# Gate products of all rows ahead of the last expert block's down product

## The chip, the cores and the metric

One core of a Trainium2 chip runs the whole program. The metric is the device time of one execution in microseconds, on that core.

## What is computed

One decoder layer on 320 rows of width 1024 (256 prompt rows and 64 sample rows): attention-like mixers, then a mixture of experts, then the per-layer input embedding, then a last norm. Everything is float32. The change touches what follows the last expert block:

```python
x = x + _moe(_rms(x, norm_moe_g[i]), router_w[i], ...)      # top 4 of 32 experts, clamped SwiGLU
gate = jax.nn.sigmoid(_rms(x, norm_ple_g[i]).astype(x.dtype) @ ple_gate_w[i])
x = x + gate * (p[i] @ ple_w[i])
...
y = _rms(x, final_norm_g)
```

`_rms` multiplies each row by one number (one over the root of its mean square) and each column by a gain. So `_rms(x) @ W` is, row by row, that number times `(x * gain) @ W`, and `(x * gain) @ W` is a sum over the parts of which `x` is made.

## The kernel before, in words

The 320 rows stand in `X` as three tiles: t = 0 and t = 1 with 128 prompt rows each, t = 2 with the 64 sample rows. The experts are walked in blocks of up to 64 rows (`SL`), one after the other, on a ring of 12 weight slots of 1 MB. A block's up and gate weights take slots 0 to 7 (four transfers of 2 MB), its down weights slots 8 to 11 (two transfers). Each body of the loop, `expert(i + 2, 2)`, does on TensorE the up product of block b, the scatter of block b-2, the gather of block b+1 and the down product of block b-1. SyncE's queue issues each transfer as soon as the semaphore `w_used` says that its slots have been read.

Scatter: a block's result `yS` holds 64 rows in 128 partitions (columns 0 to 511 of a row in partition s, columns 512 to 1023 in partition 64 + s). `SELT` holds the router's weights as a selection matrix, so `SELT^T @ yS` adds each row of the block, times its weight, to the row of `X` it belongs to.

Behind the loop stands the tail, with last_b the last block. Its up product has been done by then, its down product not. On TensorE the tail is, in this order: the sums for block last_b-1 and for the bias (`sum_slots`, `sum_bias`, L1192 and L1199) that stay open in six PSUM banks, the turn of the selection (L1093), the down product of last_b from slots 0 to 3 (L1133), its scatter into the same open banks (L1221), then for the tiles in `LAST_ORDER` = (2, 0, 1) the transposes of `X` (L568) and the products with the gate weights `wple` (L1244 for t = 2, L1232 for t = 0 and t = 1). VectorE adds the banks to `X` (L2204) and writes the transposes, times the gain, to `xT` (L2213). ScalarE takes the sums of squares (L1268), and GpSimd the power -0.5 (L453).

The rest of the tail goes over six halves (three tiles, two halves of 512 columns): ScalarE takes the sigmoid of a gate bank (L1557), VectorE multiplies it with the embedding part `pw` (L2229) and adds it to `X` (L2231). After both halves of a tile ScalarE squares the tile (L1268, or L1563 by halves for t = 1), GpSimd takes the power, VectorE scales the rows (L2236, L2243), and SyncE stores them. ScalarE and VectorE work strictly in the order written: the sigmoid of tile 0 stands behind the squares of tile 2 on ScalarE, and the products of tile 0 stand behind the last scaling of tile 2 on VectorE.

Of the kernel before, what the change touches and what calls it, by code (L numbers as in the profile page):

```python
# [12 lines left out]
P = 128  # L13
# [14 lines left out]
NE = 32  # L28
# [28 lines left out]
def build(nc, a, o):  # L57
    with ExitStack() as ctx:
# [103 lines left out]
        wple = ring[:, 8 * SLOTW:12 * SLOTW].rearrange("p (k n) -> p k n", k=KD)  # L162
# [63 lines left out]
        gT = etake(NTOK)  # L226
        bdr = xT[:, :, :].rearrange("p c t -> p (c t)")[0:NE, 0:D]
# [64 lines left out]
        TAKEN = {"pT": 1, "lexp": 2, "gT": 3}  # L292
# [5 lines left out]
        def _(sp):  # L298
# [82 lines left out]
            with sp.Fori(0, rest) as i:  # L381
                b = i + 1
                e = sp.value_load(etab[0:1, bass.ds(b + 1, 1)], min_val=0, max_val=NE - 1)
                for c in range(0, NGU, 2):
                    sp.wait_ge(sem("w_used"), used(b, c + 1))
                    load_pair(sp, e, c)
                e = sp.value_load(etab[0:1, bass.ds(b, 1)], min_val=0, max_val=NE - 1)
                for c in range(NGU, NCK, 2):
                    sp.wait_ge(sem("w_used"), used(b, c + 1))
                    load_pair(sp, e, c)  # L390
            e = sp.value_load(etab[0:1, bass.ds(last_b, 1)], min_val=0, max_val=NE - 1)
# [3 lines left out]
            w_ple = a["ple_gate_w"].rearrange("o (k p) n -> p (o k) n", p=P)  # L395
# [135 lines left out]
        def _(pe):  # L531
# [657 lines left out]
            def sum_slots(t, start, stop):  # L1189

                for h in range(2):
                    last = mm(PB[SUMB[t][h]][0:ROWS[t], :], SELT[SL * h:SL * h + SL, OFF[t]:OFF[t] + ROWS[t]],  # L1192
                              yS[SL * h:SL * h + SL, :], start=start, stop=stop, skip_group_check=True)
                return last

            def sum_bias(t):

                for n in range(2):
                    mm(PB[SUMB[t][n]][0:ROWS[t], :], gT[0:NE, OFF[t]:OFF[t] + ROWS[t]], bdr[:, 512 * n:512 * n + 512],  # L1199
                       start=False, stop=False, skip_group_check=True)  # L1200
# [6 lines left out]
            for t in (0, 2):  # L1207
                sum_slots(t, True, False)
                sum_bias(t)
            pe.wait_ge(sem("xg"), last_b + 2)  # L1210
            pe.wait_ge(sem("up"), last_b + 1)
            sum_slots(1, True, False)
            sum_bias(1)
            turn_select(last_b, 2)
            pe.wait_ge(sem("act"), last_b + 1)
            for c in range(NGU, NCK):
                down_chunk(last_b, c, c - NGU)
            pe.wait_ge(sem("selT"), last_b + 1)
            pe.wait_ge(sem("yS"), last_b + 1)
            for t, h in ((0, 0), (2, 0), (2, 1), (0, 1), (1, 0), (1, 1)):  # L1220
                last = mm(PB[SUMB[t][h]][0:ROWS[t], :], SELT[SL * h:SL * h + SL, OFF[t]:OFF[t] + ROWS[t]],  # L1221
                          yS[SL * h:SL * h + SL, :], start=False, stop=True, skip_group_check=True)
                if (t, h) in ((2, 1), (0, 1), (1, 1)):
                    last.then_inc(sem("x2_ps"), 1)

            def ple_gate(t):

                R = ROWS[t]
                pe.wait_ge(sem("xT"), 14 + 2 * t + 2)
                for n in range(2):  # L1230
                    for k in range(KD):
                        last = mm(PB[SUMB[t][n]][0:R, :], xT[:, k, OFF[t]:OFF[t] + R], wple[:, k, 512 * n:512 * n + 512],  # L1232
                                  start=(k == 0), stop=(k == KD - 1))
                    last.then_inc(sem("gate_ps"), 1)

            pe.wait_ge(sem("x1"), 8)
            turn_rows_x(2, (2, 4))
            pe.wait_ge(sem("x1"), 10)
            pe.wait_ge(sem("xT"), 14)
            turn_rows_x(0, (2, 4))  # L1240
            pe.wait_ge(sem("ple_in"), 64)
            for k in range(KD):
                for n in range(2):
                    last = mm(PB[0][64 * n:64 * n + 64, :], xT[:, k, 256:320], wple[:, k, 512 * n:512 * n + 512],  # L1244
                              start=(k == 0), stop=(k == KD - 1), skip_group_check=True)
            last.then_inc(sem("gate_ps"), 2)
# [3 lines left out]
            ple_gate(0)  # L1250
            ple_gate(1)
# [3 lines left out]
        def _(act):  # L1255
# [284 lines left out]
            take_select(last_b, 2)  # L1540
# [27 lines left out]
        def _(dve):  # L1568
# [628 lines left out]
            def add_last(i):  # L2197
# [17 lines left out]

            add_last(0)
            add_last(1)
            xT_last(0)
            xT_last(1)
            add_last(2)  # L2220
            xT_last(2)
            for i in range(3):
# [50 lines left out]
```

## Time and profile before

| | |
|---|---|
| median of 3 runs | 1320.37 us (1319.15 to 1327.6) |
| profiled execution, its own time | 1324.6 us |
| span of its trace | 1322.9 us |
| TensorE busy | 1260.6 us, 95% of the span |
| VectorE busy | 522.6 us, 40% |
| ScalarE busy | 214.6 us, 16% |
| DMA, over the span | 438.30 MB, mean 331 GB/s |
| granted TensorE clock, mean | 0.993 of full speed |

Starts are counted from the first instruction of the span. A matmul of this program stands in the trace as two records, so "x32" is 16 matmuls. Busy times of TensorE are modelled at their ends, so a start to the next start is the surer length.

### The profile page before, as it was taken

How to read it: one execution, taken by the hardware profiler on the slowest of the kernel's cores; microseconds unless marked ns; L12 is line 12 of the kernel's file. 1: busy time of each engine (PE TensorE's matmuls, PEld its weight loads, DVE VectorE, ACT ScalarE, POOL GpSimd, SP SyncE). 2: the span in 40 equal slices, each digit the busy share in tenths (PEclk: the TensorE clock that was granted, in tenths of full speed). 3: DMA queues.
4: the chain of work that ended last, by engine and by line, in shares of the span. 5: the costliest groups of instructions: out<-in, count | busy, mean ns of one | idle time of the engine just before them, and what ended most of it. 6: DMA issues, size and time to landing. Idle time of an engine off the chain costs nothing.

```text
span 1322.9 us, 17013 instructions
## 1 busy us (share of the span) xinstructions
PE 1260.6 (95%) x6271; PEld 546.7 (41%) x6271; DVE 522.6 (40%) x1148; ACT 214.6 (16%) x422; POOL 46.7 (4%) x106
## 2 busy tenths in 40 slices
PE   6999898889999999999999999999999999999997
PEld 4765687644333333333333333333333333333333
DVE  2683444745833334343333333333334333333333
ACT  2451102142111111111111111111111111111112
POOL 5100001100000000000000000000000000000000
PEclk9999999989999999999999999999999999999999
DMA  8431110346799999999999999999999999999931
GB/s 246 119 114 64 64 65 5 135 170 228 281 427 427 429 430 428 429 428 429 428 430 429 428 429 428 429 429 429 428 428 429 430 428 429 428 428 429 430 152 40
DMA packets 54485, 438.30 MB, mean 331 GB/s; under 512 B 10538, under 2 KB 17863, under 8 KB 29850
## 3 DMA queue, kind: packets, MB, share of 16 engines
q1 hardware_dynamic: 54336, 437.89, 80.0%
q8 instruction: 18, 0.29, 0.1%
q14 instruction: 9, 0.07, 0.0%
q10 hardware_dynamic: 122, 0.04, 0.0%
HBM read 432.89 MB, written 5.02 MB: 331 GB/s over the span
## 4 chain that ended last, share of the span: by engine, by line
PE 52%; DMA 41%; DVE 3%; issue 2%; ACT 1%; POOL 0%; SPq 0%; DVEq 0%; POOLq 0%; ACTq 0%
DMA ring<-in_expert_w_down 40%; PE bank L1122 12%; PE bank L1133 12%; PE bank L597 8%; PE bank L1078 2%; PE bank L773 2%; PE bank L595 2%; PE bank L1108 1%; PE bank L1232 1%; PE bank L682 1%; PE bank L694 1%; PE bank L1143 1%; PE bank L692 1%; DMA X<-in_x_sample 1%; PE bank L1086 1%
## 5 line engine op out<-in xcount | busy, mean ns | idle before, releaser
L1122 PE MATMUL bank<-ring,SC 128*64 128x512 f32 x2048 | 465.1, 598 | 13.3 <-DMA ring<-in_expert_w_gu 12.3
L1122 PEld LDWEIGHTS bank<-ring,SC 128*64 128x64 f32 x2048 | 140.4, 137 | 303.8 <-issue 267.7
L1133 PE MATMUL bank<-ring,SC 128*64 128x512 f32 x1024 | 229.9, 594 | 3.9 <-DMA ring<-in_expert_w_down 3.9
L2091 DVE TENSOR_TENSOR SC<-bank,gmoe 128x512 f32<-128x512 f32 x33 | 22.8, 692 | 464.7 <-PE bank L1086 464.6
L1133 PEld LDWEIGHTS bank<-ring,SC 128*64 128x64 f32 x1024 | 71.5, 137 | 156.4 <-issue 133.2
L2109 DVE TENSOR_TENSOR X<-X,bank 128x512 f32<-128x512 f32 x120 | 77.1, 684 | 106.1 <-PE bank L1108 105.1
L597 PE MATMUL bank<-xT,ring 128*128 128x320 f32 x384 | 112.5, 440 | 6.6 <-ACTq L1330 5.6
L1499 ACT ACTIVATE SC<-bank 128x512 f32<-128x512 f32 x33 | 19.7, 597 | 448.6 <-PE bank L1078 448.6
L1078 PE MATMUL bank<-XS,SC 128*64 128x512 f32 x396 | 90.6, 592 | 0.6 <-DVE SC L2085 0.6
L597 PEld LDWEIGHTS bank<-xT,ring 128*128 128x128 f32 x384 | 70.7, 191 | 35.9 <-ACTq L1330 7.5
L1108 PE MATMUL bank<-SC 64*128 64x512 f32 x240 | 67.7, 641 | 0.0
L2122 DVE TENSOR_TENSOR SC<-bank,bgu 128x256 f32<-128x256 f32 x128 | 48.1, 418 | 11.9 <-issue 10.8
L1078 PEld LDWEIGHTS bank<-XS,SC 128*64 128x64 f32 x396 | 28.4, 137 | 57.5 <-issue 47.4
L2113 DVE TENSOR_TENSOR X<-X,bank 64x256 f32<-64x256 f32 x120 | 49.9, 416 | 1.8
L1512 ACT ACTIVATE SC<-bank 128x512 f32<-128x512 f32 x31 | 18.5, 598 | 187.8 <-PE bank L1133 187.8
L453 POOL TENSOR_TENSOR nst<-nst,mhalf 128x1 f32<-128x1 f32 (+1 forms) x12 | 6.5, 542 | 1035.0 <-DVE nst L1594 1014.3
L1143 PE MATMUL bank<-ident,SC 128*128 128x128 f32 x256 | 36.1, 284 | 0.5 <-ACT SC L1504 0.5
L773 PE MATMUL bank<-ring,xT 128*128 128x512 f32 x64 | 33.2, 652 | 1.2 <-DVE X L1609 0.8
L1503 ACT ACTIVATE SC<-bank 128x512 f32<-128x512 f32 x32 | 19.1, 597 | 90.8 <-PE bank L1122 90.8
L1143 PEld LDWEIGHTS bank<-ident,SC 128*128 128x128 f32 x256 | 33.3, 208 | 0.7 <-ACT SC L1504 0.7
L1108 PEld LDWEIGHTS bank<-SC 64*128 64x128 f32 x240 | 18.1, 184 | 35.9 <-issue 35.9
L1516 ACT ACTIVATE SC<-SC 128x512 f32<-128x512 f32 x32 | 20.1, 630 | 68.3 <-DVE SC L2130 68.3
(478 smaller groups left out, 1019.9 us busy)
## 6 DMA issues: line engine op xcount, KB each, us to landing
ring<-in_expert_w_gu SPq DMA_DIRECT2D x128, 2048.0 KB, 23.3
ring<-in_expert_w_down SPq DMA_DIRECT2D x64, 2048.0 KB, 24.4
ring<-in_w_in SPq DMA_DIRECT2D x7, 2048.0 KB, 7.8
ring<-in_w_out SPq DMA_DIRECT2D x2, 2048.0 KB, 8.4
ring<-in_ple_gate_w SPq DMA_DIRECT2D x4, 1024.0 KB, 15.2
out_gdn_s<-Sf SPq DMA_DIRECT2D x1, 2048.0 KB, 9.4
X<-in_x_prompt SPq DMA_DIRECT2D x2, 512.0 KB, 6.4
SC<-in_ple_w SPq DMA_DIRECT2D x1, 1024.0 KB, 5.0
```

The lines of the kernel that those rows point to most:

```text
L595: ins = mm(out[0:ROWS[c], :], xT[:, k, OFF[c]:OFF[c] + ROWS[c]], w[:, k, :], start=(k == 0), stop=(k == KD - 1))
L597: ins = mm(out[:, 0:NTOK], w[:, k, c * P:c * P + P], xT[:, k, :], start=(k == 0), stop=(k == KD - 1))
L773: ins = mm(PB[0][:, :], xT[:, k, OFF[t]:OFF[t] + P], wo[:, k, 512 * n:512 * n + 512], start=(k == 0), stop=(k == KD - 1))
L1078: last = mm(PB[7][SL * h:SL * h + SL, :], SEL[:, t, :], XS[:, t, 512 * h:512 * h + 512], start=(t == 0), stop=(t == 2), skip_group_check=True)
L1108: last = mm(out[:, :], SELT[SL * h:SL * h + SL, P * t:P * t + P], yS[SL * h:SL * h + SL, :], start=True, stop=True)
L1122: last = mm(PB[j][SL * h:SL * h + SL, :], xg[:, c % 4, c // 4, :], w[:, FF * h + 512 * j:FF * h + 512 * j + 512], start=(c == 0), stop=(c ...
L1133: last = mm(PB[4][SL * h:SL * h + SL, :], act_t[:, 2 * (c - NGU) + kk, :], w[:, D * kk + 512 * h:D * kk + 512 * h + 512], start=(c == NGU ...
L1143: last = turn(PB[2 + m // 4][:, P * (m % 4):P * (m % 4) + P], hS[:, spread(m, 4)], ident[:, :])
L2091: tell(V.tensor_tensor(xg, PB[7][:, :].rearrange("p (j h s) -> p j h s", j=4, h=2), bc(gmoe[:, :, :].rearrange("p h j -> p j h"), 3, SL), ...
L2109: ins = V.tensor_tensor(dst, dst, src[0:R, :], ALU.add)
L2113: ins = V.tensor_tensor(dst, dst, src[64 * r:64 * r + 64, 0:256], ALU.add)
L2122: ins = V.tensor_tensor(out[:, 4 * i:4 * i + 4, :], PB[2 + i][:, :].rearrange("p (k h s) -> p k h s", k=4, h=2)[:, :, h, :], bgu[:, c0 + 4 ...
```

## The change

The gate product is split. `X` gets the share of all blocks but the last, is transposed and multiplied with `wple` while the last block's down product hasn't been done. Then the down product follows, and its share is added on two ways: to `X` by the scatter, as before, and to the open gate banks by transposing `yS` to `yT`, multiplying its 64 rows with `wple` (a result `zS` of 64 rows) and scattering `zS` with the same `SELT`.

On TensorE there are 26 matmuls more: four transposes of `yS`, 16 for `yT` with `wple`, and six to scatter `zS`. VectorE gets one more pass from a PSUM bank (`yT`) and six more adds to `X` (`add_part`, over all three tiles, stands beside `add_last`), ScalarE one more copy (`zS`). `wple` moves from slots 8 to 11 to slots 0 to 3 and is loaded first, as two transfers of 2 MB in the place of four of 1 MB; the last down weights go to slots 8 to 11 behind it.

```diff
-        wple = ring[:, 8 * SLOTW:12 * SLOTW].rearrange("p (k n) -> p k n", k=KD)
+        wple = ring[:, 0:4 * SLOTW].rearrange("p (k n) -> p k n", k=KD)
...
+        yT = gt.rearrange("p k s -> p (k s)").rearrange("p (j h s) -> p j h s", j=4, h=2)
+        zS = hS[:, 0:512]
...
+            for i in range(2):
+                sp.wait_ge(sem("w_used"), used(last_b, 2 * i + 1))
+                sp.dma_start(wple[:, 4 * i:4 * i + 4, :], w_ple[:, 4 * i:4 * i + 4, :]).then_inc(sem("ple_in"), 16)
             e = sp.value_load(etab[0:1, bass.ds(last_b, 1)], min_val=0, max_val=NE - 1)
-            for i in range(0, NDN, 2):
-                sp.wait_ge(sem("w_used"), used(last_b, i + 1))
-                sp.dma_start(ring[:, i * SLOTW:(i + 2) * SLOTW], w_dn[e, :, i // 2, :]).then_inc(sem(f"w_full{i}"), 16)
...
-            for i in range(NDN):
-                sp.wait_ge(sem("w_used"), used(last_b, NGU + i))
-                sp.dma_start(wple[:, 2 * i:2 * i + 2, :], w_ple[:, 2 * i:2 * i + 2, :]).then_inc(sem("ple_in"), 16)
+            for c in range(NGU, NCK, 2):
+                sp.wait_ge(sem("w_used"), used(last_b, c + 1))
+                load_pair(sp, e, c)
...
+            sum_slots(0)
+            sum_slots(2)
+            sum_bias(2).then_inc(sem("x2_ps"), 1)
+            sum_bias(0).then_inc(sem("x2_ps"), 1)
...
+            sum_slots(1)
+            sum_bias(1).then_inc(sem("x2_ps"), 1)
+
+            def gate_half(t, n):
+
+                for k in range(KD):
+                    mm(PB[SUMB[t][n]][0:ROWS[t], :], xT[:, k, OFF[t]:OFF[t] + ROWS[t]], wple[:, k, 512 * n:512 * n + 512],
+                       start=(k == 0), stop=False, skip_group_check=True)
+
+            def last_rows(t, banks):
+
+                for h in range(2):
+                    out = PB[banks[h]][0:P, :] if t < 2 else PB[banks[0]][SL * h:SL * h + SL, :]
+                    last = mm(out, SELT[SL * h:SL * h + SL, OFF[t]:OFF[t] + ROWS[t]], yS[SL * h:SL * h + SL, :],
+                              start=True, stop=True, skip_group_check=True)
+                last.then_inc(sem("x2_ps"), 1)
...
             pe.wait_ge(sem("x1"), 12)
             pe.wait_ge(sem("xT"), 16)
             turn_rows_x(1, (2, 4))
-            ple_gate(0)
-            ple_gate(1)
+            gate_half(0, 0)
+            gate_half(0, 1)
+            pe.wait_ge(sem("xT"), 18)
+            down(last_b)
+            gate_half(1, 0)
+            pe.wait_ge(sem("selT"), last_b + 1)
+            pe.wait_ge(sem("yS"), last_b + 1)
+            for j in range(4):
+                last = turn(PB[1][:, P * j:P * j + P], yS[:, P * j:P * j + P], ident[:, :])
+            last.then_inc(sem("xsT"), 1)
+            last_rows(2, (4,))
+            gate_half(1, 1)
+            pe.wait_ge(sem("xT"), 19)
+            last_rows(0, (1, 2))
+            pe.wait_ge(sem("x1"), 14)
+            for k in range(KD):
+                for n in range(2):
+                    last = mm(PB[4][SL * n:SL * n + SL, :], yT[:, k % 4, k // 4, :], wple[:, k, 512 * n:512 * n + 512],
+                              start=(k == 0), stop=(k == KD - 1), skip_group_check=True)
+            last.then_inc(sem("gate_ps"), 1)
+            pe.wait_ge(sem("x1"), 16)
+            last_rows(1, (1, 2))
+            pe.wait_ge(sem("taken"), TAKEN["zS"])
+            for t in LAST_ORDER:
+                for n in range(2):
+                    out = PB[SUMB[t][n]][0:P, :] if t < 2 else PB[0][SL * n:SL * n + SL, :]
+                    last = mm(out, SELT[SL * n:SL * n + SL, OFF[t]:OFF[t] + ROWS[t]], zS[SL * n:SL * n + SL, :],
+                              start=False, stop=True, skip_group_check=True)
+                    if t < 2:
+                        last.then_inc(sem("gate_ps"), 1)
+                if t == 2:
+                    last.then_inc(sem("gate_ps"), 2)
...
             for i in range(3):
+                if i == 2:
+                    act.wait_ge(sem("gate_ps"), 1)
+                    A(zS, PB[4][:, :], ACT.Copy).then_inc(sem("taken"), 1)
                 t = LAST_ORDER[i]
-                act.wait_ge(sem("x1"), 6 + 2 * i + 2)
+                act.wait_ge(sem("x1"), 12 + 2 * i + 2)
                 squares(t, XS[:, t, :]).then_inc(sem("ss"), 1)
...
-                act.wait_ge(sem("gate_ps"), i + 1)
+                act.wait_ge(sem("gate_ps"), i + 2)
...
+            dve.wait_ge(sem("xsT"), 19)
+            tell(V.tensor_tensor(yT, PB[1][:, :].rearrange("p (j h s) -> p j h s", j=4, h=2),
+                                 bc(pcol[:, 16:24].rearrange("p (h j) -> p j h", h=2), 3, SL), ALU.mult), "xT")
+            add_last(0, (4,))
+            add_last(1, (1, 2))
+            add_last(2, (1, 2))
```

TensorE around the last down product. In the kernel before it stands behind the turn of the selection, and its scatter (L1221) right behind it:

```order
L1093 MATMUL bank2<-ident,SC 128x128 [waits selg]
L1093 MATMUL bank2<-ident,SC 128x128 x2
L1129 ISA [waits act]
L1133 MATMUL bank4<-ring,SC 64x512 [waits w_full0]
L1133 MATMUL bank4<-ring,SC 64x512 x7
L1133 MATMUL bank4<-ring,SC 64x512 [waits w_full2]
L1133 MATMUL bank4<-ring,SC 64x512 x7
L1221 MATMUL bank5<-SC 128x512 [waits yS,selT]
L1221 MATMUL bank0<-SC 64x512
L1221 MATMUL bank1<-SC 64x512
L1221 MATMUL bank6<-SC 128x512
L1221 MATMUL bank7<-SC 128x512
```

In the changed kernel (its own line numbers: L1221 is now a half of a gate product, L1228 the scatter of the last block's rows, L1254 the transposes of `yS`):

```order
L1221 MATMUL bank5<-ring,xT 128x512 x8
L1221 MATMUL bank6<-ring,xT 128x512 x8
L1131 ISA [waits act,xT]
L1135 MATMUL bank4<-ring,SC 64x512 [waits w_full8]
L1135 MATMUL bank4<-ring,SC 64x512 x7
L1135 MATMUL bank4<-ring,SC 64x512 [waits w_full10]
L1135 MATMUL bank4<-ring,SC 64x512 x7
L1221 MATMUL bank7<-ring,xT 128x512 x8
L1254 MATMUL bank1<-ident,SC 128x128 [waits yS,selT]
L1254 MATMUL bank1<-ident,SC 128x128 x3
L1228 MATMUL bank4<-SC 64x512 x2
L1221 MATMUL bank3<-ring,xT 128x512 x8
```

The down product now stands behind the gate product of tile 0 and ahead of both halves of tile 1's. TensorE's last rows, in the kernel before, from the last transposes on:

```order
L568 MATMUL bank2<-ident,X 128x128 [waits xT,x1]
L568 MATMUL bank2<-ident,X 128x128 x3
L568 MATMUL bank4<-ident,X 128x128 x4
L1232 MATMUL bank5<-ring,xT 128x512 [waits xT]
L1232 MATMUL bank5<-ring,xT 128x512 x7
L1232 MATMUL bank6<-ring,xT 128x512 x8
L1232 MATMUL bank7<-ring,xT 128x512 [waits xT]
L1232 MATMUL bank7<-ring,xT 128x512 x7
L1232 MATMUL bank3<-ring,xT 128x512 x8
```

In the changed kernel (L1263 is `yT` with `wple`, L1272 the scatter of `zS`):

```order
L1228 MATMUL bank1<-SC 128x512 [waits xT]
L1228 MATMUL bank2<-SC 128x512
L1263 MATMUL bank4<-ring,SC 64x512 [waits x1]
L1263 MATMUL bank4<-ring,SC 64x512 x15
L1228 MATMUL bank1<-SC 128x512 [waits x1]
L1228 MATMUL bank2<-SC 128x512
L1272 MATMUL bank0<-SC 64x512 [waits taken]
L1272 MATMUL bank0<-SC 64x512
L1272 MATMUL bank5<-SC 128x512
L1272 MATMUL bank6<-SC 128x512
L1272 MATMUL bank7<-SC 128x512
L1272 MATMUL bank3<-SC 128x512
```

The gate banks 0, 5, 6, 7 and 3 are now completed all together at the very end, where each was completed by its own product. ScalarE, from its copy of `yS` on, before:

```order
L1542 ACTIVATE SC<-bank4 128x512 [waits w_used]
L1268 ACTIVATE XS,nst<-X 64x1024 [waits x1]
L1268 ACTIVATE XS,nst<-X 128x1024 [waits x1] x2
L1557 ACTIVATE SC<-bank0,nst 64x512 [waits rs,gate_ps] x2
L1268 ACTIVATE XS,nst<-X 64x1024 [waits x3]
L1557 ACTIVATE SC<-bank5,nst 128x512 [waits x3,rs,gate_ps]
L1557 ACTIVATE SC<-bank6,nst 128x512 [waits x3,rs,gate_ps]
L1268 ACTIVATE XS,nst<-X 128x1024 [waits x3]
L1557 ACTIVATE SC<-bank7,nst 128x512 [waits x3,rs,gate_ps]
L1563 ACTIVATE XS,nst<-X 128x512 [waits x3]
L1557 ACTIVATE SC<-bank3,nst 128x512 [waits x3,rs,gate_ps]
L1563 ACTIVATE XS,nst<-X 128x512 [waits x3]
```

And in the changed kernel (L1568 the copy of `yS`, L1574 that of `zS`, L1294 the squares, L1586 the sigmoids, L1592 the squares by halves):

```order
L1568 ACTIVATE SC<-bank4 128x512 [waits w_used]
L1294 ACTIVATE XS,nst<-X 64x1024 [waits x1]
L1294 ACTIVATE XS,nst<-X 128x1024 [waits x1]
L1574 ACTIVATE SC<-bank4 128x512 [waits gate_ps]
L1294 ACTIVATE XS,nst<-X 128x1024 [waits x1]
L1586 ACTIVATE SC<-bank0,nst 64x512 [waits rs,gate_ps] x2
L1294 ACTIVATE XS,nst<-X 64x1024 [waits x3]
L1586 ACTIVATE SC<-bank5,nst 128x512 [waits x3,rs,gate_ps]
L1586 ACTIVATE SC<-bank6,nst 128x512 [waits x3,rs,gate_ps]
L1294 ACTIVATE XS,nst<-X 128x1024 [waits x3]
L1586 ACTIVATE SC<-bank7,nst 128x512 [waits x3,rs,gate_ps]
L1592 ACTIVATE XS,nst<-X 128x512 [waits x3]
```

The sigmoids stand in the same order, but the copy of `zS` and the squares of tile 1 ahead of the first of them now wait for the end of TensorE's row.

## Rows read from the trace of the kernel before

**Rows 1.** The page's chain that ended last: shares of the span by engine.
```profile
PE 52%; DMA 41%; DVE 3%; issue 2%; ACT 1%; POOL 0%; SPq 0%; DVEq 0%; POOLq 0%; ACTq 0%
```

**Rows 2.** The chain in order of time, from 1220.91 on: start, us, link, instructions.
```profile
1220.91 3.68 PE bank L1133 x16
1224.74 25.50 DMA ring<-in_expert_w_down
1250.28 3.65 PE bank L1133 x16
```

**Rows 3.** Stretches of the tail: busy time and instructions by engine, clock, DMA share, GB/s.
```profile
core 0: us, PE busy (x) PEld busy (x) DVE busy (x) ACT busy (x) POOL busy (x), PEclk, DMA share, GB/s
1268.00:1272.00 4.00, 4.00 (x20) 1.15 (x16) 0.00 (x0) 0.00 (x0) 0.00 (x0) 1.00 0.34 129
1265.00:1315.00 50.00, 47.96 (x166) 19.92 (x164) 16.65 (x29) 10.99 (x19) 2.62 (x5) 1.00 0.14 51
1315.05:1322.90 7.85, 0.00 (x0) 0.00 (x0) 3.01 (x5) 1.39 (x3) 0.54 (x1) 0.77 0.18 67
```

**Rows 4.** Timeline, TensorE in the tail: start, us, line, operation, idle time before it.
```profile
1255.83 1.13 PE L1192 MATMUL bank<-SC 64*128 64x512 f32 x4
...
1256.89 1.98 PE L1199 MATMUL bank<-xT,SC 32*128 32x512 f32 x4
...
1264.63 0.55 PE L1093 MATMUL bank<-ident,SC 128*128 128x128 f32 x3
...
1265.11 7.09 PE L1133 MATMUL bank<-ring,SC 128*64 128x512 f32 x32
...
1272.98 4.01 PE L1221 MATMUL bank<-SC 64*128 64x512 f32 x12 [0.79 <-ACT SC L1542]
...
1276.46 0.71 PE L568 MATMUL bank<-ident,X 64*128 64x64 f32 x8
...
1278.41 1.07 PE L568 MATMUL bank<-ident,X 128*128 128x128 f32 x8 [1.25 <-DVE xT L2213]
...
1279.41 7.09 PE L1244 MATMUL bank<-ring,xT 128*64 128x512 f32 x32
...
1286.43 1.09 PE L568 MATMUL bank<-ident,X 128*128 128x128 f32 x8
...
1287.36 27.63 PE L1232 MATMUL bank<-ring,xT 128*128 128x512 f32 x64
```

**Rows 5.** Timeline, VectorE and ScalarE between 1259 and 1283.
```profile
1259.89 0.85 DVE L2098 TENSOR_SCALAR SC<-iota_s,posb,gateb 128x128 f32<-128x128 f32 x3
...
1272.24 0.60 ACT L1542 ACTIVATE SC<-bank 128x512 f32<-128x512 f32 x1 [6.54 <-PE bank L1133]
...
1280.29 1.27 DVE L2204 TENSOR_TENSOR X<-X,bank 128x512 f32<-128x512 f32 x2
...
1281.59 1.06 ACT L1268 ACTIVATE XS<-X 128x1024 f32<-128x1024 f32 x1 [2.81 <-DVE X L2204]
...
1282.56 0.19 ACT L1268 ACTIVATION_READ_ACCUMULATOR XS<-X 128x1 f32 x1
```

**Rows 6.** Timeline, VectorE and ScalarE from the first sigmoid on.
```profile
1289.18 1.39 ACT L1557 ACTIVATE SC<-bank,nst 64x512 f32<-64x512 f32 x2 [6.43 <-POOL nst L453]
...
1295.82 0.68 DVE L2229 TENSOR_TENSOR SC<-SC,Sf 128x512 f32<-128x512 f32 x1
...
1296.54 0.69 DVE L2231 TENSOR_TENSOR X<-X,SC 128x512 f32<-128x512 f32 x1
...
1303.47 1.06 ACT L1268 ACTIVATE XS<-X 128x1024 f32<-128x1024 f32 x1 [1.49 <-DVE X L2231]
...
1305.45 1.28 DVE L2236 SCALAR_TENSOR_TENSOR X<-X,nst,ring 128x1024 f32<-128x1024 f32 x1 [0.65 <-POOL nst L453]
...
1310.33 0.63 ACT L1563 ACTIVATE XS<-X 128x512 f32<-128x512 f32 x1 [1.49 <-DVE X L2231]
...
1315.03 0.69 ACT L1557 ACTIVATE SC<-bank,nst 128x512 f32<-128x512 f32 x1 [3.97 <-PE bank L1232]
```

More of the change, by code:

```diff
@@ L1187, in _, with sum_slots @@
             SUMB = [(5, 6), (7, 3), (0, 1)]
-            def sum_slots(t, start, stop):
+            def sum_slots(t):
                 for h in range(2):
-                    last = mm(PB[SUMB[t][h]][0:ROWS[t], :], SELT[SL * h:SL * h + SL, OFF[t]:OFF[t] + ROWS[t]],
-                              yS[SL * h:SL * h + SL, :], start=start, stop=stop, skip_group_check=True)
-                return last
+                    mm(PB[SUMB[t][h]][0:ROWS[t], :], SELT[SL * h:SL * h + SL, OFF[t]:OFF[t] + ROWS[t]],
+                       yS[SL * h:SL * h + SL, :], start=True, stop=False, skip_group_check=True)
             def sum_bias(t):
                 for n in range(2):
-                    mm(PB[SUMB[t][n]][0:ROWS[t], :], gT[0:NE, OFF[t]:OFF[t] + ROWS[t]], bdr[:, 512 * n:512 * n + 512],
-                       start=False, stop=False, skip_group_check=True)
+                    last = mm(PB[SUMB[t][n]][0:ROWS[t], :], gT[0:NE, OFF[t]:OFF[t] + ROWS[t]], bdr[:, 512 * n:512 * n + 512],
+                              start=False, stop=True, skip_group_check=True)
+                return last
             pe.wait_ge(sem("selT"), rest + 1)
@@ L1216, in _ @@
[L1216 to L1234, printed above, removed]
+            sum_slots(1)
+            sum_bias(1).then_inc(sem("x2_ps"), 1)
@@ L1236, in _ @@
             pe.wait_ge(sem("x1"), 8)
             turn_rows_x(2, (2, 4))
+            turn_select(last_b, 1)
             pe.wait_ge(sem("x1"), 10)
@@ L1240, in _ @@
             turn_rows_x(0, (2, 4))
-            pe.wait_ge(sem("ple_in"), 64)
+            pe.wait_ge(sem("ple_in"), 32)
             for k in range(KD):
                 for n in range(2):
-                    last = mm(PB[0][64 * n:64 * n + 64, :], xT[:, k, 256:320], wple[:, k, 512 * n:512 * n + 512],
-                              start=(k == 0), stop=(k == KD - 1), skip_group_check=True)
-            last.then_inc(sem("gate_ps"), 2)
+                    mm(PB[0][64 * n:64 * n + 64, :], xT[:, k, 256:320], wple[:, k, 512 * n:512 * n + 512],
+                       start=(k == 0), stop=False, skip_group_check=True)
             pe.wait_ge(sem("x1"), 12)
@@ L2195, in _, with add_part @@
             SUMB = [(5, 6), (7, 3), (0, 1)]
-            def add_last(i):
+            def add_part(i):
                 t = LAST_ORDER[i]
@@ L2204, in add_last @@
                     tell(V.tensor_tensor(dst, dst, PB[SUMB[t][n]][0:R, :], ALU.add), "x1")
+            def add_last(i, banks):
+                t = LAST_ORDER[i]
+                R = ROWS[t]
+                dve.wait_ge(sem("x2_ps"), 3 * rest + 3 + i + 1)
+                for n in range(2):
+                    src = PB[banks[n]][0:P, :] if t < 2 else PB[banks[0]][SL * n:SL * n + SL, :]
+                    dst = X[0:R, t, 512 * n:512 * n + 512]
+                    tell(V.tensor_tensor(dst, dst, src, ALU.add), "x1")
             def xT_last(i):
@@ L2214, in xT_last @@
                                          bc(pcol[:, 16 + 4 * hb:16 + 4 * hb + 4], 2, R), ALU.mult), "xT")
-            add_last(0)
-            add_last(1)
+            add_part(0)
+            add_part(1)
             xT_last(0)
+            add_part(2)
             xT_last(1)
-            add_last(2)
             xT_last(2)
+            dve.wait_ge(sem("xsT"), 19)
[4 more added lines that the diff above has]
+            add_last(2, (1, 2))
             for i in range(3):
```

14 lines of the change are left out of this document (4 added, 10 removed).

## The prediction

> **What bounds the kernel now.** I read the page's chain first: TensorE has 52% of the span and the DMA 41% [rows 1]. Followed in order of time, the chain shows where each rules. Up to 1250.28 it alternates between 25.50 us of weight transfer and 3.65 to 3.68 us of down product [rows 2]: the expert loop is paced by the weights. The step at 1250.28 is the last one in it that has a transfer as its link. The question for this change is whether TensorE stands idle in the tail for want of weights, because that idle time is what gate products set ahead of the last down product could fill. So next the stretches: the DMA stream falls to a share of 0.34 between 1268 and 1272, so it ends near 1269, and TensorE is busy for 4.00 of those 4.00 us [rows 3]. From 1265 to 1315 it is busy for 47.96 of 50.00. TensorE's own row then shows sums from 1255.83 with no idle time named, the last down product at 1265.11 with no wait ahead of it, and the waits that there are: 0.79 us for the copy of yS and 1.25 us for xT [rows 4], beside about 1 us at 1276 while VectorE adds. From 1250 on TensorE sets the time, not the stream. There is nearly nothing to fill.
>
> Last, what lies behind TensorE. Its last matmul ends at 1287.36 + 27.63 = 1315.0 [rows 4], and the span ends at 1322.9, so 7.9 us stand open behind it [rows 3]. All the other work of the last stage, the six sigmoids, products, adds and squares, starts at 1289.18 [rows 6] and runs beneath the 27.63 us of gate products. Only the last half of tile 1 comes after them.
>
> **The change, first part: TensorE's row, rebuilt.** Nothing in the loop changes, nor the bytes before its end, so I keep before's times up to 1255.83. The sums are the same twelve matmuls in another order and end at 1264.6 again (where the turn of the selection starts) [rows 4]. VectorE is free for the new add_part at 1259.89 + 0.85 = 1260.7 [rows 5]; two pairs of adds at 1.27 us each [rows 5] are done by 1263.4, so X for tiles 2 and 0 waits ready, and the adds cost nothing here. Then:
>
> - transposes of tile 2, 0.71, and the turn of the selection, 0.48 (1264.63 to 1265.11), to 1265.8; a short wait for xT, 0.3 by my estimate (before it was 1.25 while VectorE also had tile 0's adds to do, and the turn now covers most of it), to 1266.1 [rows 4];
> - transposes of tile 0, 1.00 (1278.41 to 1279.41), to 1267.1; the gate product of tile 2, 7.02 (1279.41 to 1286.43), to 1274.2; transposes of tile 1, 0.93, to 1275.1 [rows 4];
> - both halves of tile 0's gate product, 2 x 27.63/4 = 13.8, to 1288.9 [rows 4];
> - the last down product, 7.0, to 1295.9. Its weights now come last in the stream, by about 1270 [rows 3], 19 us before they are wanted, so their move costs nothing; that cover would have to go entirely before it did;
> - half of tile 1's gate product, 6.9, to 1302.8. It hides the 0.60 us copy of yS [rows 5];
> - four transposes of yS, half of the eight at 1.00, so 0.5, and the scatter of tile 2's rows, one pair of K = 64 matmuls, 1.06 (1255.83 to 1256.89), to 1304.4 [rows 4];
> - the other half of tile 1, 6.9, to 1311.3, and a pair for tile 0, 1.06, to 1312.4; yT is written under this;
> - yT with wple, 16 matmuls in the shape of tile 2's product, 7.02, to 1319.4; the pair for tile 1, 1.06, to 1320.5. It hides the copy of zS (0.60);
> - the three pairs that scatter zS, 3 x 1.06, to 1323.6.
>
> So TensorE ends at 1323.6 where it ended at 1315.0, 8.6 us later: about 7.0 for yT's product, 0.5 for the transposes, 3.2 for zS, less the two waits and the slow scatter of before (4.01 us for the six matmuls of L1221 [rows 4], that now take 3 x 1.06).
>
> The shape that no row has is a pair that splits both rows and columns of the array (the scatter of tile 2's rows and of zS to tile 2). Bounds from the nearest rows: half of a K = 64 pair, 0.5, if it runs better than the pair at 1255.83, and two matmuls that don't overlap, 1.91 (1256.89 on, four records of K = 32 in 1.98) [rows 4]. I take 1.06, the same row height. Three to four such pairs ahead of the end give -2 to +3 us.
>
> The rows show no idle time at a change of shape: from 1255.83 the sums go from a K = 64 pair to K = 32 products with starts 1.06 apart [rows 4], and what a change costs is inside these durations. The Trainium skill (TensorEngine Tiling (Array Packing), Key Properties) says instead that changing the tiling mode drains the engine. That speaks against this change, which puts the 64-row down product and the small scatters between full-size gate products. By that rule its some ten additional changes would each cost a drain for which that section states no time. The trace shows no such gap, so the sum stays.
>
> **The change, second part: what no longer runs beneath TensorE.** Before, the gate bank of tile 2 was complete at 1286.4 and tile 0's at 1301.2, so two thirds of the last stage ran under the gate products. Now all six halves are completed by zS, after 1320.5. Moreover ScalarE's order has the squares of tile 1 ahead of the first sigmoid, and those need the last add to X. That is: TensorE's last scatter of yS at 1320.5, two adds 1.27 with about 0.1 ahead of them [rows 5], 1321.9, and the squares 1282.56 + 0.19 - 1281.59 = 1.16 [rows 5], 1323.0. The first sigmoid, by then no longer waiting for zS in tile 2 (complete at 1321.6), starts at T = 1323.1.
>
> From T on nothing is hidden, and ScalarE and VectorE pass each tile to and fro. Put together from before's rows with TensorE's waits taken out [rows 6]:
>
> - from the first sigmoid to VectorE's first product of tile 0: 1295.82 - 1289.18 = 6.6 (sigmoid, four VectorE operations, squares, power, the scaling of tile 2; TensorE wasn't what ended it);
> - tile 0's two halves on VectorE: 2 x 1.41 (from 1295.82 to 1296.54 + 0.69) = 2.8, at 9.5;
> - squares of tile 0 to the end of its scaling: 1305.45 + 1.28 - 1303.47 = 3.3, at 12.7;
> - first half of tile 1 on VectorE, 1.4, at 14.1, and its square, 0.63 and a hand-over, at 14.9;
> - the sigmoid of its second half up to the end of the span: 1322.9 - 1315.03 = 7.9, at 22.8.
>
> The span ends at 1323.1 + 22.8 = 1345.9, against 1322.9: 23.0 us longer, of which 8.6 is TensorE's and the rest the stage that lost its cover (22.8 against 7.9 us open at the end). The profiled execution took 1324.6 us, 1.7 more than its span, and the changed one should take about 1347.6; against the median of 1320.4, that is 1343.4.
>
> The other edits cost nothing. The gate weights come as two transfers and earlier, and the same bytes stand in the queue. The final gain's transfer stays behind them, and is first wanted 50 us later. add_last's adds for tiles 2 and 0 run under TensorE. GpSimd's powers are the same in number.
>
> **Rivals.**
>
> *Only TensorE's extra work counts.* If the tail of ScalarE and VectorE still overlapped with the products, and only the 7.9 us behind the last matmul stayed open as now, the span would end at 1323.6 + 7.9 = 1331.5, 8.6 us later: 1329.0. For it speaks that these engines are mostly idle (16.65 and 10.99 us busy of 50 [rows 3]). Against it: in the changed order no sigmoid can start before zS's scatter. The order of the instructions decides that. 4%.
>
> *Faster: the gate products fill a wait for the last weights.* If TensorE had idled until the last pair of down weights, which the changed kernel gets near 1270, all three gate products would be free. Then half a down product (3.5), the copy of yS (0.7), the transposes and yT (0.5 + 0.9), yT with wple (7.0), and from there the 3.7 to T and 22.8: 1309.1, 13.8 us shorter, so 1306.6. It decides from some 28 us of idle time between 1250 and 1270, and the rows show TensorE busy throughout 1268 to 1272 and the down product starting at 1265.11 without a wait [rows 3, 4]. 2%.
>
> *More than forecast.* The halves of a gate product are now cut by other work; if TensorE's clock fell in a wait there, matmuls would take twice as long. Its granted clock was 1.00 from 1265 to 1315, and 0.77 only after its last matmul [rows 3]. The new waits for yT and for zS are each below 1 us, so I see no place for it, but each 7 us product at the lower of the two levels would add 7: 1350 or more. 4%.
>
> *The change doesn't do what it says*: the weights of the last block, now last in the stream, could come so late that the down product waits. That needs 19 us of delay, and would cost what goes beyond. Under 1%.
>
> **How the numbers follow.** The forecast, TensorE's 8.6 us and the uncovered stage, has 90% and the median 1343.4. Its bounds: the unseen pairs -2 to +3, the waits that I set at 0.3 and 0.1 up to 1 each, the hand-overs in the last 22.8 us within 2, and the runs of before, from 1319.15 to 1327.6, on which the median rests. I take 1337 to 1351, which leaves out the first two rivals. A measurement of this kernel can tell about 1% from no change, some 13 us. Faster by over 1% is the second rival, 0.02; within 1% the first and the lowest edge, 0.05; slower 0.93.
>
> **What would show it.** In the changed profile: TensorE without a gap over 1 us from 1264 to about 1323; the last down product near 1289 with no transfer named ahead of it; the first sigmoid near 1323, behind the squares of tile 1 and not behind zS; and 22.8 us from it to the end, in which TensorE is idle. I am wrong if the down product starts later than 1290 behind a transfer, if TensorE idled before 1264 in a way that the modelled ends hide, or if the sigmoids of tile 2 start before the squares of tile 1.

## The result, and the profile after

The changed kernel takes 1344.13 us (median of 4 runs, 1340.91 to 1348.79), the kernel before 1322.05 us (4 runs, 1319.15 to 1327.6). The ratio is 1.0174, with a 95% interval of 1.0149 to 1.0200: slower by 22 us. The profiled execution took 1348.79 us, with a span of 1347.0 us.

The page's chain that ended last, by engine, has hardly moved; it is no place to find the change:

```profile
PE 53%; DMA 40%; DVE 3%; issue 2%; ACT 1%; POOL 0%; SPq 0%; DVEq 0%; POOLq 0%; ACTq 0%
```

Its links at the end of the expert loop (start, us, link) show the same loop with the same periods as in [rows 2]:

```profile
1221.91 25.49 DMA ring<-in_expert_w_down
1247.44 3.65 PE bank L1135 x16
```

The last down product of the loop starts at 1247.44 here and at 1250.28 before. Executions reach this point between 1244 and 1254 us, whatever the tail. Most of that spread goes with falls of the granted clock in the first 360 us (before it was 0.91 from 260 to 280 and 0.83 from 280 to 300; in e11 below it was 1.00 throughout, and the loop's last down product started at 1244.16), but not all: in e8 it was 1.00 up to there too, and the start is 1246.79. So the tails are best compared from this start to the end of the span: I call this the tail's length. Before it is 1322.9 - 1250.28 = 72.6 us, in this execution 1347.0 - 1247.44 = 99.6 us.

The tail of the changed kernel in the timeline (start, us, engine, line, operation, idle time before it and what ended it), the counterpart of [rows 4] to [rows 6]:

```profile
1258.82 1.96 PE L1194 MATMUL bank<-SC 64*128 64x512 f32 x4
...
1260.71 3.78 PE L1200 MATMUL bank<-xT,SC 32*128 32x512 f32 x4
...
1266.15 1.92 PE L570 MATMUL bank<-ident,X 128*128 128x128 f32 x8
...
1276.54 13.90 PE L1221 MATMUL bank<-ring,xT 128*128 128x512 f32 x32
...
1290.37 7.09 PE L1135 MATMUL bank<-ring,SC 128*64 128x512 f32 x32
...
1297.38 7.13 PE L1221 MATMUL bank<-ring,xT 128*128 128x512 f32 x16
...
1314.01 7.09 PE L1263 MATMUL bank<-ring,SC 128*64 128x512 f32 x32
...
1322.09 2.99 PE L1272 MATMUL bank<-SC 64*64 64x512 f32 x12
...
1323.53 1.06 ACT L1294 ACTIVATE XS<-X 128x1024 f32<-128x1024 f32 x1 [1.78 <-DVE X L2243]
...
1324.58 1.38 ACT L1586 ACTIVATE SC<-bank,nst 64x512 f32<-64x512 f32 x2
...
1331.21 0.68 DVE L2274 TENSOR_TENSOR SC<-SC,Sf 128x512 f32<-128x512 f32 x1
```

TensorE now has no named wait in this stretch. The down product stands at 1290.37 without a transfer ahead of it. TensorE's last matmul ends at 1322.09 + 2.99 = 1325.1, and only 1324.58 brings the first sigmoid (it stood at 1289.18 in [rows 6], in the midst of the gate products). It comes right behind the squares of tile 1 (1323.53). From it to the end of the span are 22.4 us, with TensorE idle for 21.9 of them; before, 7.9 us stood behind the last matmul.

One thing is not in the plan. The pair at 1258.82 takes 1.96 us where the same pair took 1.13 in [rows 4], the bias matmuls behind it 3.78 in place of 1.98, and the transposes at 1266.15 1.92 in place of 1.07. The stretches by granted clock (columns: busy us and count of each engine, PEclk, DMA share, GB/s) name the reason:

```profile
core 0: us, PE busy (x) PEld busy (x) DVE busy (x) ACT busy (x) POOL busy (x), PEclk, DMA share, GB/s
1255.00:1258.80 3.80, 3.80 (x10) 1.11 (x8) 3.56 (x9) 0.08 (x1) 0.00 (x0) 1.00 1.07 448
1258.80:1268.60 9.80, 9.80 (x30) 4.84 (x31) 4.70 (x9) 0.49 (x1) 0.00 (x0) 0.51 0.79 331
```

The granted clock is 1.00 up to 1258.8 and 0.51 for the 9.8 us behind it, the lower of its two levels (1.2 and 2.4 GHz), although TensorE is busy for the whole stretch. The low level lasts from 1259.0 to 1269.2 in all, so at most 5.1 us are lost. Two more executions of the same kernel follow among the experiments; the one in which the clock stays up has a tail 4.5 us shorter.

### The profile page after: what moved, and what is told of

It reads as the page before. It is cut to its first block, busy times and chain, and to the rows that moved or that the text cites. A ratio compares the mean times of both kernels' runs of the same rounds, so it can differ in the third digit from the quotient of the medians.

```text
span 1347.0 us, 17117 instructions
## 1 busy us (share of the span) xinstructions
PE 1274.4 (95%) x6319; PEld 551.3 (41%) x6319; DVE 527.0 (39%) x1155; ACT 214.6 (16%) x423; POOL 46.5 (3%) x106
## 4 chain that ended last, share of the span: by engine, by line
PE 53%; DMA 40%; DVE 3%; issue 2%; ACT 1%; POOL 0%; SPq 0%; DVEq 0%; POOLq 0%; ACTq 0%
DMA ring<-in_expert_w_down 40%; PE bank L1124 12%; PE bank L1135 11%; PE bank L599 8%; PE bank L1080 2%; PE bank L1221 2%; PE bank L775 2%; PE bank L597 2%; PE bank L1110 1%; PE bank L684 1%; PE bank L696 1%; PE bank L1145 1%; PE bank L694 1%; DMA X<-in_x_sample 1%; PE bank L1241 1%
## 5 line engine op out<-in xcount | busy, mean ns | idle before, releaser
L2120 DVE TENSOR_TENSOR SC<-bank,gmoe 128x512 f32<-128x512 f32 x33 | 22.8, 691 | 464.7 <-PE bank L1088 464.6
L599 PEld LDWEIGHTS bank<-xT,ring 128*128 128x128 f32 x384 | 71.1, 193 | 36.0 <-ACTq L1356 7.5
```

The costliest lines, as they stand in the source:

```text
L599: ins = mm(out[:, 0:NTOK], w[:, k, c * P:c * P + P], xT[:, k, :], start=(k == 0), stop=(k == KD - 1))
```

## The experiments

All tail lengths below are from the start of the loop's last down product to the end of the span, in one profiled execution of each kernel.

| kernel | tail starts | span | tail, us | clock falls in the sums |
|---|---|---|---|---|
| before | 1250.28 | 1322.9 | 72.6 | no |
| changed | 1247.44 | 1347.0 | 99.6 | yes |
| changed, again (e7) | 1254.16 | 1349.3 | 95.1 | no |
| changed, third (e8) | 1246.79 | 1346.4 | 99.6 | yes |
| cover taken from before (e1) | 1249.16 | 1336.4 | 87.2 | no |
| changed, no share in the gate (e2) | 1245.62 | 1335.3 | 89.7 | no |
| changed, cover given back (e3) | 1245.63 | 1329.4 | 83.8 | no |
| changed, sums as before (e4) | 1244.55 | 1339.7 | 95.2 | no |
| the same, again (e11) | 1244.16 | 1339.3 | 95.1 | no |
| the same, third (e12) | 1248.94 | 1344.1 | 95.2 | no |
| before, loads as changed (e5) | 1244.34 | 1318.6 | 74.3 | no |
| before, gaps filled (e6) | 1246.37 | 1317.5 | 71.1 | no |
| changed, six bias matmuls in a row (e9) | 1251.27 | 1348.9 | 97.6 | yes |
| the same, again (e10) | 1244.25 | 1341.8 | 97.6 | yes |

### e1: the cover alone taken away, from the kernel before

```diff
             for i in range(6):
                 t, m = LAST_ORDER[i // 2], i % 2
                 R = ROWS[t]
-                act.wait_ge(sem("gate_ps"), i + 1)
+                act.wait_ge(sem("gate_ps"), 6)
```

> The kernel before with one added wait: ScalarE starts no sigmoid before all gate banks are complete. TensorE's work is untouched. Theory (the lost cover is a cost of its own): TensorE still ends near 1315.0, the first sigmoid starts there, and 22.8 us follow in place of 7.9, so the span is 14.9 us longer than before, about +1.1%. Rival (only TensorE's extra matmuls count, ScalarE and VectorE have slack): within 1 us of before.

Measured: 1340.44 us against 1322.43, ratio 1.0126 (1.0068 to 1.0184). In its timeline TensorE and ScalarE meet here:

```profile
1311.55 2.31 PE L1232 MATMUL bank<-ring,xT 128*128 128x512 f32 x5
...
1313.89 1.39 ACT L1557 ACTIVATE SC<-bank,nst 64x512 f32<-64x512 f32 x2 [32.28 <-PE bank L1232]
```

TensorE ends at 1313.9, the first sigmoid starts at 1313.89, and 22.5 us follow. The tail is 87.2 us, 14.6 longer than before's, with not one matmul more. The theory said 14.9. The rival, by which ScalarE and VectorE have slack because they are mostly idle, is refuted: their chain of sigmoid, product, add, squares, power and scaling is 22.5 us long from end to end, and it costs nothing only while TensorE has other work.

### e2: the changed kernel without yT's product and zS

ScalarE's copy of zS goes with them. What is left out is the last block's share in the gate.

```diff
-            gate_half(1, 1)
+            gate_half(1, 1).then_inc(sem("gate_ps"), 7)
             pe.wait_ge(sem("xT"), 19)
             last_rows(0, (1, 2))
-            pe.wait_ge(sem("x1"), 14)
-            for k in range(KD):
...
-            last.then_inc(sem("gate_ps"), 1)
             pe.wait_ge(sem("x1"), 16)
             last_rows(1, (1, 2))
-            pe.wait_ge(sem("taken"), TAKEN["zS"])
-            for t in LAST_ORDER:
...
```

> The changed kernel without the product of yT with wple, without zS and its scatter; the transposes of yS and yT are kept. It leaves out the last block's share in the gate. Theory (ScalarE's squares of tile 1 decide when the last stage starts, zS is hidden behind them): the 16 matmuls, 7.0 us, go, but the pair for tile 1 now waits about 1.4 us for the adds of tile 0 that they had covered, so the end comes 5.7 us earlier than in the changed kernel; the 3.2 us of the zS scatter give nothing. Rival (all of TensorE's extra work counts): 10.2 us earlier.

Measured: 1339.17 us, ratio to before 1.0123 (1.0071 to 1.0175). The tail is 89.7 us, against 95.1 for the changed kernel at full clock: 5.4 us shorter. The theory said 5.7, the rival 10.2. The place where the difference goes:

```profile
1306.73 1.13 PE L1229 MATMUL bank<-SC 64*128 64x512 f32 x4
...
1309.34 1.13 PE L1229 MATMUL bank<-SC 64*128 64x512 f32 x4 [1.48 <-DVE X L2226]
...
1312.88 1.38 ACT L1569 ACTIVATE SC<-bank,nst 64x512 f32<-64x512 f32 x2
```

The pair at 1309.34 waits 1.48 us for VectorE's adds of tile 0, which the 7 us product had covered. And the first sigmoid still comes behind tile 1's adds and squares. So the scatter of zS, 3.0 us on TensorE, costs nothing on the path: it lies beside two adds and a pass of squares.

### e3: the same work with the cover given back

```diff
             down(last_b)
-            gate_half(1, 0)
...
             last_rows(2, (4,))
-            gate_half(1, 1)
...
-            for t in LAST_ORDER:
-                for n in range(2):
...
+            add_z(2, 0)
+            add_z(2, 1).then_inc(sem("gate_ps"), 2)
+            add_z(0, 0).then_inc(sem("gate_ps"), 1)
+            add_z(0, 1).then_inc(sem("gate_ps"), 1)
+            for n in range(2):
+                gate_half(1, n)
+                add_z(1, n).then_inc(sem("gate_ps"), 1)
```

> The changed kernel with the same matmuls in another order: the last down product, yT's product and zS for tiles 2 and 0 come ahead of both halves of tile 1's gate product, each of which is followed by its own zS matmul. Theory: TensorE ends about 2 us later than in the changed kernel (the copy of yS, yT and the adds of tile 2 are waited for), near 1325.6, but only 7.9 us stay open behind it, so the span is 12.4 us shorter than the changed kernel's and about 10.6 us longer than before's (+0.8%). Rival (the cover is worth nothing): no shorter than the changed kernel, 1 to 2 us longer.

Measured: 1335.31 us (median of 10 runs) against 1322.43, ratio 1.0093 (1.0065 to 1.0121). Its timeline:

```profile
1303.23 2.13 PE L1270 MATMUL bank<-SC 64*64 64x512 f32 x8
...
1305.29 7.13 PE L1221 MATMUL bank<-ring,xT 128*128 128x512 f32 x16
...
1305.72 1.38 ACT L1588 ACTIVATE SC<-bank,nst 64x512 f32<-64x512 f32 x2
...
1312.36 1.12 PE L1270 MATMUL bank<-SC 64*128 64x512 f32 x2
1313.41 7.13 PE L1221 MATMUL bank<-ring,xT 128*128 128x512 f32 x16
...
1320.47 1.12 PE L1270 MATMUL bank<-SC 64*128 64x512 f32 x2
1321.63 0.69 ACT L1588 ACTIVATE SC<-bank,nst 128x512 f32<-128x512 f32 x1 [1.17 <-PE bank L1270]
```

The first sigmoid is at 1305.72, and both halves of tile 1's gate product (1305.29 and 1313.41) run beneath it. The last matmul ends at 1321.6, and 7.8 us follow it, as before the change. The tail is 83.8 us: 11.3 shorter than the changed kernel's 95.1 (the theory said 12.4) and 11.2 longer than before's (10.6). So half of the change's cost is undone by its order alone. The 11.2 us that remain are about what the added matmuls take here: 7.0 for yT's product, 0.5 for the transposes and 4.2 for zS, 11.7 together. The scatter of zS took 3.0 in the changed kernel; here tile 1's two matmuls stand alone, and each takes 1.05 us (1312.36 to 1313.41), as long as a pair that shares the array. TensorE's end came 2.7 us later than in the changed kernel, not the theory's 2, and this is part of it. This order is faster than the changed kernel's (the interval of its ratio to before ends at 1.0121, the other's begins at 1.0149) and still slower than the kernel before.

### e5: the load order alone

```diff
-        wple = ring[:, 8 * SLOTW:12 * SLOTW].rearrange("p (k n) -> p k n", k=KD)
+        wple = ring[:, 0:4 * SLOTW].rearrange("p (k n) -> p k n", k=KD)
...
-                down_chunk(last_b, c, c - NGU)
+                down_chunk(last_b, c, c)
```

with SyncE's queue as in the change.

> The kernel before with only the change's load order: gate weights first into slots 0 to 3, the last block's down weights last into slots 8 to 11. The down product stays where it was, about 15 us behind the start of the last down product of the loop. This shows the largest wait that gate products set ahead of it could fill. Theory (TensorE sets the time from there on): the last two transfers land about 14 and 19 us behind that point, so the first half of the down product doesn't wait and the second waits 1 us or less; time within 1 us of before. Rival (the down product would wait for its weights, and the gate products fill that wait): a gap of 5 us or more on TensorE behind a transfer, and the run longer by as much.

Measured: 1321.06 us against 1320.98, ratio 1.0011 (0.9986 to 1.0036). TensorE around the down product:

```profile
1244.34 3.65 PE L1133 MATMUL bank<-ring,SC 128*64 128x512 f32 x16 [0.19 <-DMA ring<-in_expert_w_down]
...
1258.68 0.55 PE L1093 MATMUL bank<-ident,SC 128*128 128x128 f32 x3
1259.45 3.65 PE L1133 MATMUL bank<-ring,SC 128*64 128x512 f32 x16 [0.22 <-DMA ring<-in_expert_w_down]
1264.34 3.65 PE L1133 MATMUL bank<-ring,SC 128*64 128x512 f32 x16 [1.23 <-DMA ring<-in_expert_w_down]
```

With the weights of the last block at the very end of the stream and its down product where it always was, TensorE waits 0.22 and 1.23 us for them. The tail grows by 1.7 us. That is the whole of the wait that gate products set ahead of the down product can fill, and the load order of the kernel before doesn't even have it. The theory's 1 us was slightly low; the rival's 5 us is refuted.

### e6: before's own gaps filled with its own work

```diff
             sum_slots(1, True, False)
-            sum_bias(1)
             turn_select(last_b, 2)
...
+            sum_bias(1, (0,))
             pe.wait_ge(sem("selT"), last_b + 1)
             pe.wait_ge(sem("yS"), last_b + 1)
...
+            last_scatter(((0, 0), (2, 0), (2, 1), (0, 1)))
+            sum_bias(1, (1,))
...
             turn_rows_x(2, (2, 4))
+            last_scatter(((1, 0), (1, 1)))
             pe.wait_ge(sem("x1"), 10)
```

> The kernel before with its own idle time filled by its own work: the two bias matmuls of tile 1 move into the wait for the copy of yS and behind the first scatters, and tile 1's scatter between the transposes of tiles 2 and 0. No work is added. Theory (of the tail's waits of TensorE some 2.3 us can be had without the split): the tail, from the start of the last down product of the loop to the end of the span, falls from 72.6 us to about 70.3; in the medians 0.2%, less than they can tell. Rival (these waits lie beside others and nothing comes of it): 72.6 again.

Measured: 1321.83 us (12 runs) against 1320.98 (23 runs), ratio 1.0001 (0.9975 to 1.0027): no difference that the times can tell. In the profile the tail is 71.1 us, 1.5 shorter, of the 2.3 expected:

```profile
1266.31 1.12 PE L1199 MATMUL bank<-xT,SC 32*128 32x512 f32 x2
...
1267.36 3.18 PE L1224 MATMUL bank<-SC 64*128 64x512 f32 x8
1270.47 1.12 PE L1199 MATMUL bank<-xT,SC 32*128 32x512 f32 x2
...
1272.07 1.07 PE L1224 MATMUL bank<-SC 64*128 64x512 f32 x3
...
1273.07 1.09 PE L568 MATMUL bank<-ident,X 128*128 128x128 f32 x8
```

One bias matmul at 1266.31 fills the wait for the copy of yS, and tile 1's scatter at 1272.07 most of the wait for xT. Some of the missing 0.8 us lies in the scatter: cut in two, its six matmuls take 3.11 (1267.36 to 1270.47) and 1.00 us (1272.07 to 1273.07), against 3.48 in one piece (1272.98 to 1276.46 in [rows 4]). This is the only kernel here with a shorter tail than before's, by one execution, and it isn't shown to be faster.

### e4 and e7 to e12: the granted clock in the sums

e7 and e8 are the changed kernel as it is.

> The changed kernel as it is, once more, for its granted clock. Theory (the fall to 0.5 at 1258.8 belongs to one execution): the clock stays 1.00 from the last down product of the loop to TensorE's last matmul, and this stretch up to the end of the span is 94.7 us in place of 99.6. Rival (the changed tail brings the fall about): the fall is there again and the tail 99.6 us.

> The changed kernel a third time, same expectations as for the second: a tail of 94.7 us with the clock at 1.00, or 99.6 us with a stretch at 0.5.

e7 took 1351.08 us, e8 1348.14. In e7 the clock stays up in the sums, and there the pieces have the lengths of [rows 4]:

```profile
1254.16 3.65 PE L1135 MATMUL bank<-ring,SC 128*64 128x512 f32 x16 [0.21 <-DMA ring<-in_expert_w_down]
...
1265.54 1.13 PE L1194 MATMUL bank<-SC 64*128 64x512 f32 x4
1266.60 1.98 PE L1200 MATMUL bank<-xT,SC 32*128 32x512 f32 x4
...
1269.90 1.06 PE L570 MATMUL bank<-ident,X 128*128 128x128 f32 x8 [0.21 <-DVE xT L2252]
```

and at the end of its row:

```profile
1307.19 1.07 PE L1228 MATMUL bank<-SC 64*64 64x512 f32 x4
1308.20 7.13 PE L1221 MATMUL bank<-ring,xT 128*128 128x512 f32 x16
...
1324.40 2.99 PE L1272 MATMUL bank<-SC 64*64 64x512 f32 x12
...
1326.89 1.38 ACT L1586 ACTIVATE SC<-bank,nst 64x512 f32<-64x512 f32 x2
```

Its tail is 95.1 us, as the theory had it. e8 has the fall again at the same place, and 99.6 us. So neither theory holds as put: the fall is no accident of one execution, and it isn't always there.

The changed kernel differs in this place by the order of the sums: four bias matmuls with K = 32 stand in a row, where before two did. e4 puts them back, and e9 makes the row six long (the flags that open and close a bank are swapped to match, not shown):

```diff
# e4, e11, e12
             sum_slots(0)
+            sum_bias(0)
             sum_slots(2)
-            sum_bias(2).then_inc(sem("x2_ps"), 1)
-            sum_bias(0).then_inc(sem("x2_ps"), 1)
+            sum_bias(2).then_inc(sem("x2_ps"), 2)
```

```diff
# e9, e10
             sum_bias(2).then_inc(sem("x2_ps"), 1)
             sum_bias(0).then_inc(sem("x2_ps"), 1)
...
-            sum_slots(1)
-            sum_bias(1).then_inc(sem("x2_ps"), 1)
+            sum_bias(1)
+            sum_slots(1).then_inc(sem("x2_ps"), 1)
```

> The changed kernel with the sums for tiles 0 and 2 in the order of the kernel before: each pair of slot matmuls followed by its two K = 32 bias matmuls, not four of these in a row. Theory (the granted clock of 0.5 from 1258.8 to 1268.6 in the changed kernel's profile belongs to that one execution): times within 1 us of the changed kernel's runs. Rival (the four K = 32 matmuls in a row bring it about): the clock stays 1.00 there in this kernel and the runs are up to 4.9 us shorter.

e4: 1347.43 us (4 runs, 1341.44 to 1351.01), ratio 1.0192 (1.0140 to 1.0245), no shorter in the times than the changed kernel. Its profile shows no fall and a tail of 95.2 us.

> The changed kernel with the bias of tile 1 ahead of its slots, so that all six K = 32 bias matmuls stand in a row (5.7 us). For the fall of the granted clock in the sums, seen in 2 of 5 executions with four of them in a row and in 0 of 5 with two. If the row of K = 32 matmuls brings it about, it should come here at least as often, with a tail of 99 us or more. If it is chance, it comes seldom, and the tail is 95 us.

> The same kernel with six K = 32 matmuls in a row, a second execution: a fall and 99 us or more if the row causes it, else 95 us.

e9 took 1350.61 us, e10 1343.58. Both show the fall. e9's bias matmuls and the pair behind them:

```profile
1258.88 5.99 PE L1201 MATMUL bank<-xT,SC 32*64 32x512 f32 x12
1264.80 2.08 PE L1194 MATMUL bank<-SC 64*128 64x512 f32 x4
...
1268.35 1.92 PE L570 MATMUL bank<-ident,X 128*128 128x128 f32 x8
```

```profile
1258.90:1262.00 3.10, 3.10 (x9) 1.09 (x8) 2.86 (x8) 0.00 (x1) 0.00 (x0) 1.00 1.03 436
1262.00:1272.00 10.00, 10.00 (x37) 5.12 (x37) 5.53 (x10) 0.49 (x1) 0.00 (x0) 0.66 0.76 320
```

The clock is 1.00 over the first half of the row and 0.66 on average from 1262 to 1272. The tail is 97.6 us in both executions, 2.5 longer than without a fall, where I had put 99 or more. The stretch at the low level is shorter here: some 7 us (1263.9 to 1270.7 in e9), against 10 in the changed kernel (1259.0 to 1269.2).

> The changed kernel with the sums in the order of before, a second execution. If the row of K = 32 matmuls causes the fall: none here, tail 95.2 us. If it is chance, a fall can come here too.

> The same, a third execution: no fall and 95.2 us if the row of K = 32 matmuls is the cause.

e11: 1341.08 us, no fall, 95.1. e12: 1345.90 us, no fall, 95.2.

Counted together over the profiled executions: with six in a row the clock fell in 2 of 2, with four in a row in 2 of 5 (the changed kernel three times, e2 and e3), with two in a row in 0 of 7 (before, e1, e4, e5, e6, e11, e12). That points to the row of K = 32 matmuls, but seven executions against seven are few. It is not settled, and e4's own times don't show the gain. Nor does every execution of the changed kernel have the fall: its two shortest, of 1340.91 and 1341.91 us, would have had to start a tail of 99.6 us at 1239.5 and 1240.5 (spans are 1.8 us shorter than times), and no profiled execution here starts it before 1244.16.

## Why the prediction was right

The forecast was 1343.4 us in a range of 1337 to 1351, and the median is 1344.13. As a difference, 23.0 us were forecast and 22.1 measured, on a median of before that has moved from 1320.4 (3 runs) to 1322.05 (4 runs). That the totals meet within 1 us is in part luck: with e7 and e8 the six executions of the changed kernel have a median of 1347.2, and the longest, 1351.08, lies at the range's upper edge. The tail is the better test. Against the tail of e7, where the clock stays up, its steps compare so, counted from the start of the loop's last down product:

| step | predicted | measured in e7 |
|---|---|---|
| last matmul ends | 1323.6 - 1250.3 = 73.3 us | 1324.40 + 2.99 - 1254.16 = 73.2 us |
| first sigmoid starts | 1323.1 - 1250.3 = 72.8 us | 1326.89 - 1254.16 = 72.7 us |
| from it to the end | 22.8 us | 1349.3 - 1326.89 = 22.4 us |
| tail longer by | 23.0 us | 95.1 - 72.6 = 22.5 us |

- **What bounds the tail.** That TensorE and not the stream sets the time from 1250 on is shown by e5: with the weights as late as they can come, all waits for them are under 1.5 us.
- **TensorE's row.** 8.6 us later were forecast, 73.2 - 64.7 (1315.0 - 1250.3) = 8.5 measured. The wait for xT, an estimate of 0.3, is 0.21. The shape that no row had, a pair that splits rows and columns, takes 1.01 from its start to the next (1307.19 to 1308.20 in e7), for the 1.06 of a K = 64 pair that I took. The scatter of zS takes 2.99 for 3.2. One reading was wrong: the prediction has about 1 us of waiting at 1276 in the kernel before, and [rows 4] name none there; the sum doesn't use it.
- **The lost cover.** 14.9 us were forecast for it (22.8 in place of 7.9 open at the end); e1 has 14.6 for the cover alone, and e3 gets back 11.3 us of the changed kernel's tail by order alone, against 12.4: besides the waits at the joints, 0.79 us for yS and 0.44 for the adds of tile 2, it pays about 1 us for the two zS matmuls that stand alone.
- **That the squares of tile 1, not zS, hold back the first sigmoid.** e2 takes away 10 us of TensorE's work and gains 5.4.
- **The rival of a filled wait.** It asked for some 28 us of idle time between 1250 and 1270, more than that stretch holds, so it was excluded before any run; e5 shows how little there is, 1.5 us.
- **What I had wrong.** The rival *more than forecast* named a fall of the clock and found no place for it. There was one, in the sums and not in the waits at which I looked, and it cost 4.5 us (99.6 against 95.1) in two of three profiled executions. I had called the sums "the same twelve matmuls in another order" and given that order no cost. The runs differ more than that among themselves (1340.91 to 1348.79), so the times don't show this cost.
- **Changes of the tiling mode.** The Trainium skill (TensorEngine Tiling (Array Packing), Key Properties) says that such a change drains the engine. I had said that the traces show no gap at a change. No idle time is named there, but the starts do show a small cost. Eight matmuls in the down product's shape take 3.43 us where the same shape follows (1246.92 to 1250.35 in e7, below), and its 16 take 7.01, not 6.86, where another shape follows (1290.37 to 1297.38 in the changed kernel). Half a gate product takes 7.06 ahead of a K = 64 pair (1308.20 to 1315.26 in e7), against 6.9 on average in one run (27.63/4). That is about 0.15 us at such a change; the sum hardly missed it, because the durations that it took from before have changes of shape at their ends too.

```profile
1246.92 3.60 PE L1124 MATMUL bank<-ring,SC 128*64 128x512 f32 x16
1250.35 3.60 PE L1135 MATMUL bank<-ring,SC 128*64 128x512 f32 x16
...
1315.26 1.13 PE L1228 MATMUL bank<-SC 64*128 64x512 f32 x4
```

## What to carry to other kernels

Before moving work ahead of a late transfer, read whether the engine ever waits for it: here the wait was 0 us, 1.5 at most under the worst load order, and the split that was to fill it added 10.5 us of matmuls. And before gathering several small results into one common last step, add up the chain on the other engines that each early result used to start; it may be idle by its busy share and still be 22 us long end to end. When an extra step can't be avoided, complete the early tiles first and let the largest product of the last tile run over their chain, as e3 does.

## What the runs showed of the hardware

The granted TensorE clock fell to its lower level for 10 us (0.51 over 9.8 of them) in a stretch in which TensorE was busy throughout, behind a row of matmuls that use 32 of the 128 rows: in 2 of 2 profiled executions with six of them in a row (there it fell within the row), 2 of 5 with four, 0 of 7 with two. A busy TensorE by the profile is thus no proof that the clock holds. What exactly brings the fall about stays open.

Two matmuls with K = 64 on different halves of the array's rows took 1.06 us together, and one that stood alone between full-size products took 1.05 (e3, 1312.36 to 1313.41): here half the rows cost as much alone as two such matmuls side by side.

Where the shape of the matmuls changed, the next start came about 0.15 us later than inside a row of one shape (7.01 for the 16 matmuls of a down product against twice 3.43 for eight in its shape).
